# Four local edits in a one-core hybrid layer: the norm's weight row, the first gather, the last two experts

## The chip, the cores and the metric

The kernel runs on one core of a Trainium2 chip. The metric is the device time of one execution in microseconds. The kernel before has a median of 1229.29 us over 3 runs (1228.64 to 1230.97).

## The reference

One layer on 256 tokens of width 1024, all in fp32:

```python
h = rms_norm(x, mix_norm)
proj = h @ w_in                       # 1024 -> u | v | z | xBC | dt | gate_a | gate_b
y_a = sgu_branch(proj[u, v])          # chunk-causal gMLP
y_b = mamba2_branch(proj[z], proj[xBC], proj[dt], ...)
merged = sigmoid(gate_a) * (y_a @ w_branch_a) + sigmoid(gate_b) * (y_b @ w_branch_b)
x = x + merged @ w_out
x = x + moe_ffn(rms_norm(x, ffn_norm))    # top 4 of 32 experts, hidden 1024, clamped SwiGLU
x = x + sigmoid(rms_norm(x, ple_norm) @ w_ple_gate) * (p @ w_ple_proj)
return rms_norm(x, final_norm)
```

Each of the 32 experts has w1 (1024 x 2048) and w2 (1024 x 1024) in fp32, 12 MB together.

## The kernel before, in words

Tokens lie on partitions in two tiles (t = 0, 1) of 128. Five instruction streams are written out by hand and meet only in semaphores; the order in the source is the order on the engine. There is no scheduler.

**Head.** SP loads the norm's weight row (4 KB, one partition), the two tiles of x, and then the input projection's weights in halves of 1 MB. ScalarE (ACT) squares a tile with a running sum and takes the root (L1315, L1318). TensorE (PE) multiplies a row of ones with the weight row (L755), which puts the row on all partitions in two PSUM banks, between two stretches of matmuls whose result nobody reads (`keep_busy`, L747). VectorE (DVE) multiplies x by the inverse root and by those banks (L1642). PE transposes the result in four units ("xT", t, h) of four 128x128 blocks (L699). ACT copies each unit out as the high part `a_hi` (L1344), VectorE subtracts to get the low part `a_lo` (L1625). `a_hi` lies in the memory of `x`, so all of x must have been read before it is written. Each weight is split likewise: ACT rounds (L1307), GpSimd (POOL) subtracts (L669). The convolution's part of the projection ("xbc") then runs in groups of 8 matmuls per term: L777 (high x high), L787 (low activations), L782 (low weights). From there to the router, PE works through projections, branches and merge.

**Router and first gather.** VectorE turns the router's ranks into one-hot selections (`select`, L1937). PE gathers the up to 64 chosen rows per expert as a matmul of x with the selection (`gather`, L982, 8 k-tiles by 2 token tiles into bank YB), VectorE multiplies by the norm's weight (`take_gathered`, L1942), and expert 0 begins.

**Experts.** The weights come in 6 chunks of 2 MB per expert, (e, 0) to (e, 3) of w1 and (e, 4), (e, 5) of w2, into 9 slots. SP issues chunk g when chunk g-9 has been used (`chunk_used`). Chunks 0 to 5 are issued while the branches still run, 6 to 8 when the last part of the output projection is done (`wait_filled(sp, ("wo", 1, 1))`), chunk 9 when expert 0's first chunk has been used. Per expert PE does `units_of` (w1, L1032, bias L1038), the turn of the activation (L1061), the scatter of an earlier expert's output into four accumulators (L1002), the turn of its selection (L1009) and `rows_out` (w2, L1070) into bank YB, which ACT copies to memory (L1499, L1522).

**The last two experts** share an order of their own, `last_two`: chunks arrive as (30, 0 to 3), (31, 0 to 3), (30, 4), (30, 5), (31, 4), (31, 5). After that come the last scatter (L1167), the per-layer gate (L1280 and after) with weights that SP loads once (31, 4) has landed (L624), and the final norm.

## Time and profile before

| what | value |
|---|---|
| median of 3 runs | 1229.29 us |
| the profiled execution's own time | 1227.98 us |
| its span | 1226.2 us |
| TensorE busy | 1167.1 us (95%) |
| VectorE / ScalarE / GpSimd busy | 394.3 / 224.8 / 45.1 us |
| moved by DMA | 459.60 MB, 375 GB/s on average |
| chain that ended last | PE 68%, DMA 27%, VectorE 2%, ScalarE 2% |
| expert chunks, issue to landing | 36.0 us (median) |

The chain is followed back from the last instruction to what released it each time. A busy PE does not mean that PE sets the pace: where PE and DMA run side by side, the chain names DMA only in the stretches where PE waited for a landing. The span is 1.8 us shorter than the execution's own time, and that execution is 1.3 us below the median.

### The profile page before, as it was taken

The numbers are of one execution on the slowest core, as the hardware profiler recorded it, in microseconds if no ns is written. First come the engines' busy times: TensorE is split into PE (matmuls) and PEld (weight loads), VectorE is DVE, ScalarE is ACT, GpSimd is POOL, SyncE is SP. The second block draws the span as 40 slices with busy tenths as digits, with TensorE's granted clock in tenths as the row PEclk, the third lists the DMA queues.
The fourth block names the chain that finished last, engine by engine and source line by source line (L and its number), as shares of the span: only waits on it lengthen the run. The fifth ranks groups of instructions, "written<-read, shape, count | busy, mean of one in ns | idle before, by whom it ended". The sixth has DMA issues, their size and how long they took to land.

```text
span 1226.2 us, 14127 instructions
## 1 busy us (share of the span) xinstructions
PE 1167.1 (95%) x5773; PEld 586.7 (48%) x5773; DVE 394.3 (32%) x716; ACT 224.8 (18%) x338; POOL 45.1 (4%) x32
## 2 busy tenths in 40 slices
PE   9999999999999999999998989899999999999997
PEld 8988888874343443434332423233343333233336
DVE  2679954653221232122121212212222121212127
ACT  5766654350000000000000000000000000000017
POOL 6600000010000000000000000000000000000000
PEclk9999999999999999999999999999999999999999
DMA  8655478789999999999999999999999999999991
GB/s 271 203 172 206 137 275 334 266 304 403 430 427 427 429 428 428 429 428 428 429 428 429 430 429 428 429 426 428 427 427 428 428 428 428 429 428 427 428 391 46
DMA packets 62382, 459.60 MB, mean 375 GB/s; under 512 B 7385, under 2 KB 16993, under 8 KB 37506
## 3 DMA queue, kind: packets, MB, share of 16 engines
q1 hardware_dynamic: 62338, 458.95, 91.0%
q8 instruction: 35, 0.57, 0.2%
q14 instruction: 9, 0.07, 0.0%
HBM read 457.87 MB, written 1.06 MB: 374 GB/s over the span
## 4 chain that ended last, share of the span: by engine, by line
PE 68%; DMA 27%; DVE 2%; ACT 2%; issue 1%; ACTq 0%; SPq 0%; DVEq 0%
PE bank L1032 22%; DMA wring<-in_w_dram 15%; PE bank L1070 13%; DMA vz<-in_w_dram 12%; PE bank L712 5%; PE bank L714 5%; PE bank L713 5%; PE bank L993 4%; PE bank L1002 3%; PE bank L1038 2%; PE bank L777 1%; PE bank L782 1%; PE bank L787 1%; PE bank L699 1%; PE bank L1061 1%
## 5 line engine op out<-in xcount | busy, mean ns | idle before, releaser
L1032 PE MATMUL bank<-wring,hT 128*64 128x512 f32 x1360 | 310.4, 599 | 21.0 <-DMA wring<-in_w_dram 17.5
L1032 PEld LDWEIGHTS bank<-wring,hT 128*64 128x64 f32 x1360 | 94.1, 137 | 210.6 <-issue 171.9
L1985 DVE TENSOR_SCALAR xbcT<-bank 128x512 f32<-128x512 f32 x32 | 22.1, 692 | 526.4 <-PE bank L1038 526.4
L1070 PE MATMUL bank<-wring,xbcT 128*64 128x512 f32 x672 | 150.7, 595 | 7.3 <-DVE xbcT L2004 6.3
L1494 ACT ACTIVATE xbcT<-xbcT 128x512 f32<-128x512 f32 x32 | 20.2, 630 | 489.3 <-DVE xbcT L1985 489.3
L1070 PEld LDWEIGHTS bank<-wring,xbcT 128*64 128x64 f32 x672 | 46.5, 137 | 101.4 <-issue 91.7
L1632 DVE TENSOR_TENSOR blk_lo<-blk,blk_hi 128x2048 fp32r<-128x2048 f32 x32 | 73.0, 2287 | 39.5 <-ACT blk_hi L1309 39.5
L1032 PE MATMUL bank<-vz,hT 128*64 128x512 f32 x336 | 78.7, 599 | 7.1 <-DMA vz<-in_w_dram 7.1
L1499 ACT ACTIVATE xbcT<-bank 128x512 f32<-128x512 f32 x31 | 18.5, 597 | 352.5 <-PE bank L1070 352.5
L1032 PE MATMUL bank<-blk,hT 128*64 128x512 f32 x352 | 79.7, 594 | 3.2 <-DMA blk<-in_w_dram 3.2
L1070 PE MATMUL bank<-blk,xbcT 128*64 128x512 f32 x320 | 72.6, 595 | 3.1 <-DVE xbcT L2004 3.1
L712 PE MATMUL bank<-blk_hi,a_lo 128*128 128x512 f32 x192 | 75.5, 393 | 0.1
L714 PE MATMUL bank<-blk_lo,a_hi 128*128 128x512 f32 x192 | 74.8, 389 | 0.0
L713 PE MATMUL bank<-blk_hi,a_hi 128*128 128x512 f32 x192 | 74.7, 389 | 0.0
L1309 ACT ACTIVATE blk_hi<-blk 128x2048 fp32r<-128x2048 f32 x32 | 61.1, 1917 | 73.8 <-DMA blk<-in_w_in_dram 44.4
L1002 PE MATMUL bank<-xbcT 64*128 64x512 f32 x248 | 61.6, 615 | 0.7 <-ACT xbcT L1522 0.7
L2006 DVE COPY xbcT<-bank 128x256 f32<-128x256 f32 x32 | 13.4, 420 | 138.2 <-PE bank L1009 138.2
L1032 PEld LDWEIGHTS bank<-blk,hT 128*64 128x64 f32 x352 | 24.9, 137 | 54.3 <-issue 46.8
L1032 PEld LDWEIGHTS bank<-vz,hT 128*64 128x64 f32 x336 | 22.3, 136 | 51.2 <-issue 38.8
L993 PE MATMUL bank<-hT,ga 128*128 128x128 f32 x240 | 46.4, 275 | 0.0
L993 PE MATMUL bank<-xbcT,ga 128*128 128x128 f32 x240 | 46.3, 275 | 0.0
L1070 PEld LDWEIGHTS bank<-blk,xbcT 128*64 128x64 f32 x320 | 22.3, 137 | 48.4 <-issue 44.3
(300 smaller groups left out, 1215.2 us busy)
## 6 DMA issues: line engine op xcount, KB each, us to landing
wring<-in_w_dram SPq DMA_DIRECT2D x129, 2048.0 KB, 36.0
blk<-in_w_dram SPq DMA_DIRECT2D x42, 2048.0 KB, 35.5
vz<-in_w_dram SPq DMA_DIRECT2D x21, 2048.0 KB, 35.9
blk<-in_w_in_dram SPq DMA_DIRECT2D x28, 1024.0 KB, 5.2
blk<-in_w_branch_a_dram SPq DMA_DIRECT2D x4, 1024.0 KB, 5.5
blk<-in_w_branch_b_dram SPq DMA_DIRECT2D x4, 1024.0 KB, 8.1
blk<-in_w_out_dram SPq DMA_DIRECT2D x4, 1024.0 KB, 5.2
x<-in_x_dram SPq DMA_DIRECT2D x4, 512.0 KB, 5.3
```

Source lines behind the costliest of these rows:

```text
L712: mm(out, lhs[1], rhs[0], start=start, stop=False)
L713: mm(out, lhs[0], rhs[0], start=False, stop=False)
L714: return mm(out, lhs[0], rhs[1], start=False, stop=stop)
L993: last = mm(bank[:, k * P:(k + 1) * P], xp[:, t, (4 * h + k) * P:(4 * h + k + 1) * P], sel[t], start=(t == 0), stop=(t == TT - 1))
L1002: last = mm(ACC[t][dh][:, :], selgT[dh * SLOTS:(dh + 1) * SLOTS, t, :], y_sb[dh * SLOTS:(dh + 1) * SLOTS, :], start=False, stop=True, skip ...
L1032: last = mm(bank[dh * SLOTS:(dh + 1) * SLOTS, :], xgT[:, k, :], at(c)[:, kk * 2 * F + off + dh * W:kk * 2 * F + off + (dh + 1) * W], start ...
L1038: return mm(bank[:, :], esel[:, :], b1_pair[:, g * W:(g + 1) * W], start=False, stop=True, skip_group_check=True)
L1070: last = mm(YB[dh * SLOTS:(dh + 1) * SLOTS, :], units[:, kk * P + c * SLOTS:kk * P + (c + 1) * SLOTS], at(W1C + c)[:, kk * D + dh * W:kk * ...
L1309: fn(high(i), blk[:, i % NB, :], ACT.Copy).then_inc(blk_high, 1)
L1494: fn(sig_sb, g_sb, ACT.Sigmoid, scale=ALPHA).then_inc(msig_done, 1)
L1632: tt(blk_lo[:, i % NB, :], blk[:, i % NB, :], high(i).bitcast(FP32), ALU.subtract).then_inc(nat_low, 1)
L1985: ts(g_sb, GLU[:, :], LIMIT, None, ALU.min).then_inc(g_done, 1)
```

## The change

Four edits, with no change to what is computed:

1. The norm's weight row is loaded onto all 128 partitions by its DMA (512 KB written in place of 4 KB), between the two tiles of x. The two matmuls L755 go, and the two stretches of `keep_busy` become one of twelve matmuls. x goes into `ga` at first (`x_first`), so that `a_hi` can be written while the second tile is still being read; ACT and VectorE take up the transposed units one by one.
2. The router's gather is written in two halves of four k-tiles into two banks (YB, TB), and VectorE takes each half apart. It waits for the copy of the turned gates, which held TB.
3. Expert 30's `units_of` carries three quarters of expert 31's gather between its chunks; the last quarter follows it.
4. Expert 31's rows go into bank LIN, its first w2 chunk ahead of expert 30's scatter, and its last chunk is loaded in two DMAs.

```diff
-        mix_row = z[0:1, 0, :]
+        mix_gain = z[:, 0, :]
+        x_first = ga
...
-            load(mix_row, mix_norm, mix_loaded)
-            for t in range(TT):
-                load(x[:, t, :], x_in[0, t * P:(t + 1) * P, :], x_loaded[t])
+            for t in range(TT):
+                load(x_first[:, t, :], x_in[0, t * P:(t + 1) * P, :], x_loaded[t])
+                if t == 0:
+                    load(mix_gain, vec(mix_norm), mix_loaded)
...
+                elif g < NCH * E - 1:
+                    load(slots[g % NSLOT], chunk_src(*LAST_TWO[g - NCH * (E - 2)]), loaded[g % NSLOT])
                 else:
-                    load(slots[g % NSLOT], chunk_src(*LAST_TWO[g - NCH * (E - 2)]), loaded[g % NSLOT])
+                    for k in range(2):
+                        part = slice(k * RW2 // 2 * D, (k + 1) * RW2 // 2 * D)
+                        load(slots[g % NSLOT][:, part], chunk_src(E - 1, NCH - 1)[:, part], last_half[k])
...
-            keep_busy(idle_bank, 6, halves[:], halves[:])
+            keep_busy(idle_bank, 12, halves[:], halves[:])
             pe.wait_ge(consts, 2)
-            pe.wait_ge(mix_loaded, 16)
-            for h in range(HALVES):
-                last = mm(banks[(6 + h + BANK_SHIFT) % BANKS][:, :], ones[0:1, :], mix_row[:, h * W:(h + 1) * W], start=True, stop=True)
-            last.then_inc(gain_spread, 1)
-            keep_busy(idle_bank, 6, halves[:], halves[:])
...
+                    if first and RW1 * c == KT // 2:
+                        pe.wait_ge(xg_done, 1)
...
-            def rows_out(units, at, arrived, between=None):
+            def rows_out(units, at, arrived, between=None, to=YB, halved=False):
 
                 for c in range(W2C):
-                    arrived(W1C + c)
+                    if not (halved and c):
+                        arrived(W1C + c)
                     for kk in range(RW2):
+                        if halved and c and kk % 2 == 0:
+                            pe.wait_ge(last_half[kk // 2], 16)
...
-                units_of(first, *stream(first), 0)
-                gather(last_chosen)
+                def rows_between(c):
+
+                    gather(last_chosen if c == 0 else lambda: None, range(2 * c, 2 * c + 2))
+
+                units_of(first, *stream(first), 0, between=rows_between)
+                gather(lambda: None, range(6, KT))
...
-                pe.wait_ge(y_copied, first + 1)
-                scatter(lambda: None)
-                selected(GLU)
+                def first_scattered(c):
+
+                    pe.wait_ge(y_copied, first + 1)
+                    scatter(lambda: None)
+                    selected(GLU)
+
                 pe.wait_ge(actT_done, second + 1)
-                rows_out(actT_last, *stream(second))
+                rows_out(actT_last, *stream(second), between=first_scattered, to=LIN, halved=True)
...
+                pe.wait_ge(gateT_done, 1)
...
-            gather(first_ready)
+            first_ready()
+            for h, bank in enumerate((YB, TB)):
+                for k in range(4):
+                    for t in range(TT):
+                        last = mm(bank[:, k * SLOTS:(k + 1) * SLOTS], xp[:, t, (4 * h + k) * P:(4 * h + k + 1) * P],
+                                  sel[t][:, 0:SLOTS], start=(t == 0), stop=(t == TT - 1))
+                last.then_inc(first_rows if h == 0 else gathered, 1)
...
-            split(0, [0])
-            act.wait_ge(xn_done, 2 * TT)
-            high_parts("xT", a_hi)
+            for t in range(TT):
+                for h in range(2):
+                    if (t, h) == (1, 1):
+                        split(0, [0])
+                    name = ("xT", t, h)
+                    wait_filled(act, name)
+                    fn(a_hi[:, 4 * h:4 * h + 4, t * P:(t + 1) * P], seg4(bank_of(name)[:, :]), ACT.Copy).then_inc(act_high, 1)
...
-            take_y(E - 1)
+            act.wait_ge(chunk_used, NCH * E)
+            fn(y_sb, LIN[:, :], ACT.Copy).then_inc(y_copied, 1)
...
-            dve.wait_ge(gain_spread, 1)
-            for t in range(TT):
+            dve.wait_ge(mix_loaded, 16)
+            for t in range(TT):
+                if t:
+                    first_low(0)
                 dve.wait_ge(root_done, t + 1)
                 link(nc.vector.reciprocal(rstd[:, t:t + 1], rstd[:, t:t + 1]))
                 for h in range(HALVES):
                     cols = slice(h * W, (h + 1) * W)
-                    stt(v[:, t, cols], x[:, t, cols], rstd[:, t:t + 1], banks[(6 + h + BANK_SHIFT) % BANKS][:, :], ALU.mult,
+                    stt(v[:, t, cols], x_first[:, t, cols], rstd[:, t:t + 1], mix_gain[:, cols], ALU.mult,
                         ALU.mult).then_inc(xn_done, 1)
-            low_parts("xT", a_hi, a_lo, 0)
+            for n in range(1, 4):
+                first_low(n)
```

The first rows on ScalarE, before (`a_hi` is the high part of a transposed unit, `blk_hi1` that of a weight half):

```order
L1315 ACTIVATE u,ssq<-x 128x1024
L1318 ACTIVATE rstd<-ssq,eps 128x1
L1315 ACTIVATE u,ssq<-x 128x1024
L1318 ACTIVATE rstd<-ssq,eps 128x1
L1307 ACTIVATE blk_hi1<-blk 128x8x128
L1344 ACTIVATE a_hi<-bank6 128x4x128
L1344 ACTIVATE a_hi<-bank7 128x4x128
L1344 ACTIVATE a_hi<-bank0 128x4x128
L1344 ACTIVATE a_hi<-bank1 128x4x128
```

and now:

```order
L1339 ACTIVATE u,ssq<-ga 128x1024
L1342 ACTIVATE rstd<-ssq,eps 128x1
L1339 ACTIVATE u,ssq<-ga 128x1024
L1342 ACTIVATE rstd<-ssq,eps 128x1
L1377 ACTIVATE a_hi<-bank6 128x4x128
L1377 ACTIVATE a_hi<-bank7 128x4x128
L1377 ACTIVATE a_hi<-bank0 128x4x128
L1331 ACTIVATE blk_hi1<-blk 128x8x128
L1377 ACTIVATE a_hi<-bank1 128x4x128
```

The first weight half's rounding has moved from ahead of all four copies to a place ahead of the fourth.

PE from expert 30's second w2 chunk to the end of expert 31, before (bank6 is YB, banks 0 to 3 the accumulators):

```order
L1070 MATMUL bank6<-wring,xbcT 64x512 x8
L1002 MATMUL bank0<-xbcT 128x512
L1002 MATMUL bank1<-xbcT 128x512
L1002 MATMUL bank2<-xbcT 128x512
L1002 MATMUL bank3<-xbcT 128x512
L1009 MATMUL bank4<-ident,xbcT 128x128 x2
L1070 MATMUL bank6<-wring,hT 64x512 x16
```

and now (bank5 is LIN):

```order
L1080 MATMUL bank6<-wring,xbcT 64x512 x8
L1080 MATMUL bank5<-wring,hT 64x512 x8
L1004 MATMUL bank0<-xbcT 128x512
L1004 MATMUL bank1<-xbcT 128x512
L1004 MATMUL bank2<-xbcT 128x512
L1004 MATMUL bank3<-xbcT 128x512
L1011 MATMUL bank4<-ident,xbcT 128x128 x2
L1080 MATMUL bank5<-wring,hT 64x512 x8
```

The eight matmuls of chunk (31, 4) now stand ahead of expert 30's scatter; those of (31, 5) stay behind it.

## Rows read from the trace of the kernel before

**Rows 1.** The page, part 2: what the DMA engines moved, 40 slices.

```profile
GB/s 271 203 172 206 137 275 334 266 304 403 430 427 427 429 428 428 429 428 428 429 428 429 430 429 428 429 426 428 427 427 428 428 428 428 429 428 427 428 391 46
```

**Rows 2.** Chain that ended last, in order of time: start us, us, what.

```profile
1.38 2.93 PE bank L747 x12
4.31 3.71 PE bank L755 x4
8.02 2.86 PE bank L747 x12
10.88 2.57 PE bank L699 x12
13.47 1.19 ACT a_hi L1344 x2
14.71 1.22 PE bank L777 x8
...
17.85 0.96 PE bank L777 x8
...
1109.56 37.13 DMA vz<-in_w_dram
```

**Rows 3.** Timeline, first 30 us: start us, us, engine, line, operation [idle before <-releaser].

```profile
1.21 0.84 SPq L512 DMA_DIRECT2D x<-in_x_dram  x2
...
4.94 1.06 ACT L1315 ACTIVATE u<-x 128x1024 f32<-128x1024 f32 x1 [2.01 <-DMA x<-in_x_dram]
...
7.48 0.29 ACT L1318 ACTIVATE rstd<-ssq,eps 128x1 f32<-128x1 f32 x1
...
8.05 0.16 DVE L1639 RECIPROCAL rstd<-rstd 128x1 f32<-128x1 f32 x1 [5.16 <-PE bank L755]
8.25 1.41 DVE L1642 SCALAR_TENSOR_TENSOR vz<-x,rstd,bank 128x512 f32<-128x512 f32 x2
...
9.28 1.06 ACT L1307 ACTIVATE blk_hi<-blk 128x1024 fp32r<-128x1024 f32 x1 [1.50 <-DMA blk<-in_w_in_dram]
...
14.10 1.29 DVE L1625 TENSOR_TENSOR a_lo<-bank,a_hi 128x512 fp32r<-128x512 f32 x2 [0.16 <-ACT a_hi L1344]
...
15.68 16.59 POOL L669 TENSOR_TENSOR blk_lo<-blk,blk_hi 128x1024 fp32r<-128x1024 f32 x7 [2.91 <-ACT blk_hi L1307]
```

**Rows 4.** Line L699 (transposes): count, duration ns min/median/max, first and last start.

```profile
L699 PE MATMUL bank<-ident,vz x32: 270/273/421, 10.7 to 207.5; 128*128 128x128 f32 x32
```

**Rows 5.** Windows of 2 us; the last three numbers are clock, DMA share, GB/s.

```profile
282.00:284.00 2.00, 2.00 (x12) 0.81 (x10) 1.69 (x7) 0.00 (x0) 0.00 (x0) 1.00 1.07 360
284.00:286.00 2.00, 2.00 (x12) 0.86 (x10) 0.00 (x0) 0.00 (x0) 0.00 (x0) 1.00 0.69 254
```

**Rows 6.** Timeline of SP's queue, 195 to 345 us: issues of expert chunks.

```profile
267.69 22.11 SPq L548 DMA_DIRECT2D wring<-in_w_dram  x4
```

**Rows 7.** Chain that ended last, around expert 0's start.

```profile
274.30 3.79 PE bank L982 x32
278.09 0.83 issue
278.92 13.10 PE bank L1032 x60
```

**Rows 8.** Timeline, 255 to 300 us: VectorE's copy of the turned gates.

```profile
274.16 0.41 DVE L1954 COPY hT<-bank 32x256 f32<-32x256 f32 x1
```

**Rows 9.** Timeline of PE, 1130 to 1197 us.

```profile
1141.84 3.65 PE L1032 MATMUL bank<-wring,hT 128*64 128x512 f32 x16 [1.24 <-DMA wring<-in_w_dram]
...
1176.67 3.65 PE L1070 MATMUL bank<-wring,xbcT 128*64 128x512 f32 x16
1181.02 1.99 PE L1002 MATMUL bank<-xbcT 64*128 64x512 f32 x8 [0.70 <-ACT xbcT L1522]
...
1183.31 7.09 PE L1070 MATMUL bank<-wring,hT 128*64 128x512 f32 x32
```

**Rows 10.** Timeline of SP's queue, after 1000 us: the first gate weight loads.

```profile
1181.59 0.93 SPq L512 DMA_DIRECT2D vz<-in_w_ple_gate_dram  x2
```

More of the change, by code:

```diff
@@ L320, in build @@
         mix_loaded = sem("mix_loaded")
-        gain_spread = sem("gain_spread")
+        first_rows = sem("first_rows")
+        last_half = [sem(f"last_half{k}") for k in range(2)]
         ssm_loaded = sem("ssm_loaded")
@@ L1026, in units_of @@
                 xgT = xgT_of[0 if alone else 1 - side]
-                pe.wait_ge(xg_done, j + 1 + (not alone and side == 1))
+                if first:
+                    pe.wait_ge(first_rows, 2)
+                else:
+                    pe.wait_ge(xg_done, j + 1 + (not alone and side == 1))
                 def inner(c, kk, bank, off):
@@ L1062, in turned_units @@
                 last.then_inc(actT_filled, 1)
-            def rows_out(units, at, arrived, between=None):
+            def rows_out(units, at, arrived, between=None, to=YB, halved=False):
                 for c in range(W2C):
-                    arrived(W1C + c)
+                    if not (halved and c):
+                        arrived(W1C + c)
                     for kk in range(RW2):
+                        if halved and c and kk % 2 == 0:
+                            pe.wait_ge(last_half[kk // 2], 16)
                         for dh in range(2):
-                            last = mm(YB[dh * SLOTS:(dh + 1) * SLOTS, :], units[:, kk * P + c * SLOTS:kk * P + (c + 1) * SLOTS],
+                            last = mm(to[dh * SLOTS:(dh + 1) * SLOTS, :], units[:, kk * P + c * SLOTS:kk * P + (c + 1) * SLOTS],
                                       at(W1C + c)[:, kk * D + dh * W:kk * D + (dh + 1) * W],
@@ L1314, in _ @@
                 act.wait_ge(x_loaded[t], 16)
-                fn(u[:, t, :], x[:, t, :], ACT.Square, accum_out=ssq[:, t:t + 1]).then_inc(ssq_done, 1)
+                fn(u[:, t, :], x_first[:, t, :], ACT.Square, accum_out=ssq[:, t:t + 1]).then_inc(ssq_done, 1)
                 act.wait_ge(ssq_done, t + 1)
@@ L1635, in _, with first_low @@
             tt(dsel[:, :], ident[0:2 * HEADS, 0:HEADS], ident[0:2 * HEADS, HEADS:2 * HEADS], ALU.add).then_inc(small_set, 1)
-            dve.wait_ge(gain_spread, 1)
+            def first_low(n):
+                t, h = divmod(n, 2)
+                dve.wait_ge(act_high, n + 1)
+                cols = (slice(None), slice(4 * h, 4 * h + 4), slice(t * P, (t + 1) * P))
+                name = ("xT", t, h)
+                tt(a_lo[cols], seg4(bank_of(name)[:, :]), a_hi[cols].bitcast(FP32), ALU.subtract).then_inc(empty(name), 1)
+            dve.wait_ge(mix_loaded, 16)
             for t in range(TT):
+                if t:
+                    first_low(0)
                 dve.wait_ge(root_done, t + 1)
@@ L1958, in _ @@
                 cp(onehot[rows, 0:E], ident[rows, rows])
-            dve.wait_ge(gathered, 1)
-            take_gathered()
+            for h, (bank, done) in enumerate(((YB, first_rows), (TB, gathered))):
+                dve.wait_ge(done, 1)
+                tt(xgT_of[0][:, 4 * h:4 * h + 4, :], bank[:, 0:4 * SLOTS].rearrange("p (k s) -> p k s", k=4),
+                   fgain[:, 4 * h:4 * h + 4].unsqueeze(2).to_broadcast([P, 4, SLOTS]),
+                   ALU.mult).then_inc(xg_done if h else first_rows, 1)
             for t in range(TT):
```

## The prediction

> **What bounds the kernel now.** I read the page's DMA line first. The reader is to see that the expert stream runs flat from the eleventh slice to the last but one: 426 to 430 GB/s, slice after slice [rows 1]. A stretch that flat is DMA at its limit, although PE is busy 95% of the span. The chain that ended last agrees late in the stream: one step of it is 37.13 us of DMA that ends at 1146.69 [rows 2], the landing of chunk (30, 3). So three things can move the end: when the flat stretch begins, gaps in it, and what is left after its last chunks land. Edits 1 and 2 bear on the first two, edits 3 and 4 on the third.
>
> When does it begin? Chunks 6 to 8 are issued when the output projection is done (the row at 267.69 begins with chunk 8) [rows 6]. Up to there the chain is PE from 14.71 us on, group of matmuls behind group of matmuls [rows 2], so an earlier start of "xbc" moves the stream by as much. A gap stands right behind: in 282 to 286 us DMA moves 360 and then 254 GB/s [rows 5]. Against 428 that is 2 x 68/428 + 2 x 174/428 = 0.3 + 0.8 = 1.1 us lost. It is the wait for chunk 9, which goes out only when expert 0, begun at 278.92 [rows 7], has used its first chunk, 16 of 60 records in 13.10 us or 3.5 us later; chunks 6 to 8 have run out by then.
>
> **Edit 1, the head.** Before, the chain is keep-busy 2.93, the row's matmuls 3.71, keep-busy 2.86, twelve transposes 2.57, two high copies 1.19, then "xbc" at 14.71 [rows 2]. VectorE had waited 5.16 us for the row's matmuls [rows 3]. These go. What is late next?
> - Landings. x's first tile lands at 4.9 [rows 3]; issued one DMA sooner (0.84 for two, so 0.4 each) it lands at 4.5 to 4.9. The weight row now brings 512 KB; at about 420 GB/s that is 1.25 us, so it lands at 5.8 to 6.2 and the second tile at 7.1 to 7.5. No row shows this load in this place.
> - Square to root took (7.48 + 0.29 - 4.94)/2 = 1.4 us a tile [rows 3]. First root at 6.0 to 6.4, first norm (1.41 for two halves [rows 3]) done at 7.6 to 8.0; second root at 8.5 to 8.9.
> - ACT's first two high copies (0.6 each [rows 2]) end at 9.7 to 10.1. VectorE's first low part (1.29/2 = 0.65 [rows 3]) now stands ahead of the second tile's norm: low part to 9.8 to 10.2, reciprocal 0.2, first half of the norm 0.7: 10.7 to 11.1.
> - The third unit's four transposes at 2.57/12 = 0.21 us each take 0.85: 11.6 to 12.0. Its copy 0.6, then the rounding of the first weight half (1.06 [rows 3]) that now stands ahead of the fourth copy, then that copy 0.6: 13.9 to 14.3. The weight half itself lands 1 to 1.3 us later than at 9.28 [rows 3], by 10.6, and is not waited for.
>
> "xbc" would begin 0.4 to 0.8 us sooner. POOL gives part of it back: its first subtraction waits for that rounding, now done at 13.3 instead of 10.3, and one takes 16.59/7 = 2.37 us [rows 3], so the second low part is ready at 18.0. PE asks for it after four groups, 1.06 + 3 x 0.96 = 3.9 us [rows 2] from 13.9, at 17.8: 0.2 us. The small loads behind the weight row come about 1.3 us later too; ACT and POOL have room there, since PE wants the fifth weight half only at 14.7 + 4 x 5.8 = 38 us. Value 0.4 us gained. Bounds from the nearest rows: all 3.71 of the row's matmuls gained above; below, a loss, if PE's clock is lower where "xbc" begins (a rival).
>
> **Edit 2, the first gather.** It starts at 274.16 + 0.41 = 274.57 instead of 274.30 [rows 7, 8], since it now waits for the gates' copy: 0.3 lost. Its 32 records take 3.6 us as before, but the first half is through VectorE while the second runs, so the 0.83 us between last matmul and expert 0 goes [rows 7]. Expert 0 starts at about 278.2, 0.7 sooner, and chunk 9 is issued 0.7 sooner, inside the gap of 1.1. Value 0.7; bounds 0 (no gap of that cause) and 1.1 (the gap).
>
> **Edit 3.** PE stood 1.24 us idle before each of expert 30's later chunks [rows 9], and a quarter of the gather is about 0.9 us, so three quarters cost nothing there and 2.7 us leave the stretch behind them. But they are not collected: VectorE's chain to the activation stays, and whatever PE gains must wait for the next landings. PE takes up (30, 5) at 1176.67 [rows 9], and a chunk of 2.1 MB takes 4.9 us at 428 GB/s: six of those after 1146.69 is 1176.1, so it had hardly landed. (31, 4) landed just before 1181.59, where SP, which waits for it, issues the gate's loads [rows 10]. Value 0; bounds 0 and 0.7 (the other wait named below).
>
> **Edit 4.** Before, PE waited 0.70 us for the copy of expert 30's rows, began the scatter at 1181.02 and had no wait until the rows of 31 were done at 1190.4 [rows 9]: 9.4 us of work. After, the same work begins with (31, 4). PE is done with (30, 5) at 1180.3, must wait for the landing at about 1181.55, and then has 9.4 us ahead. The last chunk, 4.9 us behind, lands at 1186.4 and is asked for at 1187.2, so loading it in halves buys nothing. Against the stream this end is 0.5 us later. Bounds: 0.7 gained (the copy's wait gone, were (31, 4) there) and 0.6 lost.
>
> The reader who knows the page DMA: Bandwidth & Descriptors of the Trainium skill (section "Why a DMA increments its semaphore by 16 and not by 1") finds there that up to 16 engines finish a DMA independently and the wait is for all. By that rule the last engine counts, however much the others have moved, which speaks against edit 4; by a mean rate over all engines, seven steps of 4.9 after 1146.69, (31, 4) would be there at 1181.0 and the edit would cost nothing. SP's row, a real waiter on that chunk, decides for the first.
>
> **The sum.** -0.4 - 0.7 + 0 + 0.5 = -0.6 us against the profiled execution, 1227.98 (span 1226.2 and 1.8 around it), which gives 1227.4. That execution was 1.3 below the median 1229.29; on the median's scale I predict 1228.7.
>
> **Rivals.**
> - *The clock.* The transposes of the head took 421 ns, later ones 273 [rows 4], and 0.21 us apart against 0.11: PE's head ran on the lower of its two levels (1.2 and 2.4 GHz), though the granted clock reads 1.00, and it had risen by 14.71, after PE had been busy without a break since 1.38. After, PE stands idle about 2 us before the third unit and 2 before "xbc". If it is still at 1.2 GHz then, each group of 8 costs 0.96 more. Three groups: 1228.7 + 2.9 = 1231.6. From four on it is slower by more than the bound. For it: the gaps are new. Against: they are short and follow twelve matmuls on all rows; PE's 1.24 us gaps in the experts cost it no pace, 3.65 us for 16 records [rows 9]. TensorE: Matmul & The Clock Gate of the Trainium skill (Part 1, the HAM clock gate) says that the lower clock is the default and sustained activity releases it; by that rule the new order could also rise sooner.
> - *The clock, the other way.* It rises at the end of the unbroken keep-busy near 7.2 us. The third unit's transposes then take 0.44 instead of 0.85: 0.4 more, 1228.3.
> - *The tail is not held by (31, 4).* If PE finds it landed, the copy's 0.7 is gained where I charge 0.5: 1227.5. For it: PE was busy then, so none of its rows shows the landing. Against: SP's issue.
> - *The stream does not start sooner.* The gap is the queue's own and the head's gain is eaten by later loads: only the 0.5 stays, 1229.8.
>
> **How the numbers follow.** My forecast 0.44, clock low 0.10, clock early 0.22, tail free 0.12, stream fixed 0.12. The range for 8 in 10 covers all but the low clock's far end and adds the spread of a median of this kernel: 1226.9 to 1231.0. I take 0.2%, 2.5 us, as what can be told from no change. None of the faster cases reaches it alone; two together, with the head's upper bound, might: 0.07. The low clock does from four groups on, and unforeseen waits might: 0.09. Within: 0.84.
>
> **What would show it.** Right: "xbc" begins at 13.8 to 14.3 with the next groups at 0.96; expert 0 starts 0.7 sooner counted from the last output projection; the gap near 284 is about 0.4; PE idles about 1.2 us ahead of (31, 4) and the last rows end 9.4 us after its landing. Wrong: groups of 1.9 us at the start of "xbc"; a weight row that lands after 7 us; the chain passing from SP's queue to something else in the experts; (31, 4) used without a wait.

## The result: slower by 2.9 us

| kernel | median | runs | ratio, 95% interval |
|---|---|---|---|
| before | 1228.71 us | 12 | 1 |
| after | 1231.61 us | 12 | 1.0018 [1.0010, 1.0026] |
| after, timed a second time | 1231.42 us | 12 | 1.0026 [1.0013, 1.0038] |

The forecast was 1228.7, range 1226.9 to 1231.0: the time lies outside, on the side of the rival with the low clock (1231.6). The two medians are 2.9 us apart; the ratios, which pair runs of the same rounds, make it 2.2 us [1.2, 3.2] and 3.2 us [1.6, 4.7]. With twelve runs the kernel before has a median 0.6 below the 1229.29 of three runs on whose scale the forecast was put; on the new scale the forecast would be 1228.1. The profiled execution of after took 1231.88 us, its span is 1230.1, so it is 3.9 us longer than that of before.

The DMA line of the page of after is as flat as before from the eleventh slice on [rows 1]: the stream runs at the same rate, only later.

```profile
GB/s 281 207 169 209 137 250 357 245 303 406 428 429 427 427 428 427 430 427 428 429 429 428 428 429 428 428 427 428 426 429 427 427 427 429 428 426 428 427 377 37
```

**The head.** The timeline of PE in the kernel after, first 20 us (start us, us, engine, line, operation, [idle before <-what ended it]):

```profile
1.37 4.51 PE L754 MATMUL bank<-halves 128*128 128x128 f32 x24 [1.37 <-DVE halves L1643]
7.59 1.23 PE L706 MATMUL bank<-ident,vz 128*128 128x128 f32 x8 [1.71 <-DVE vz L1680]
11.45 1.94 PE L706 MATMUL bank<-ident,vz 128*128 128x128 f32 x8 [2.63 <-DVE vz L1680]
14.66 2.07 PE L779 MATMUL bank<-a_hi,blk_hi 128*128 128x256 f32 x8 [1.27 <-ACT a_hi L1377]
16.53 1.91 PE L789 MATMUL bank<-a_lo,blk_hi 128*128 128x256 f32 x8
18.24 1.16 PE L784 MATMUL bank<-a_hi,blk_lo 128*128 128x256 f32 x8
```

The same view of the kernel before, its first and its fourth group of "xbc":

```profile
14.71 1.22 PE L777 MATMUL bank<-a_hi,blk_hi 128*128 128x256 f32 x8 [0.69 <-ACT a_hi L1344]
...
17.69 1.12 PE L777 MATMUL bank<-a_hi,blk_hi 128*128 128x256 f32 x8
```

The chain of after has the fourth group as

```profile
19.40 0.96 PE bank L779 x8
```

and windows of 1 us of after (the last three numbers are granted clock, DMA share, GB/s):

```profile
11.00:12.00 1.00, 0.55 (x3) 0.56 (x4) 1.00 (x3) 0.00 (x0) 0.00 (x0) 0.76 1.10 347
12.00:13.00 1.00, 1.00 (x7) 0.99 (x5) 0.66 (x2) 0.43 (x1) 0.00 (x0) 0.50 1.12 343
...
18.00:19.00 1.00, 1.00 (x10) 1.00 (x8) 0.00 (x0) 1.00 (x2) 1.00 (x2) 0.83 1.10 342
```

The reader is to see four things. The 24 records of the products that nobody reads take 4.51 us where 24 at the old pace would be 5.86 [twice 2.93, rows 2]: the clock rises from 1.2 to 2.4 GHz inside them. Then PE idles 1.71 us, 2.63 us and 1.27 us, with 1.23 and 1.94 us of transposes between. Between 11 and 12 us the granted clock falls (0.76 over that window), and from 12 to 18 us it reads 0.50, the lower level. So "xbc" begins at 14.66, no later than before (14.71), but its first three groups take 2.07, 1.91 and 1.16 us, where in the same view of before they take 1.22, 1.12 and 1.12. A row of the timeline ends after the next has begun; in the chain of waits, where nothing is counted twice, a group at full pace is 0.96. There the fourth group begins at 19.40 instead of 17.85 [rows 2]: 1.55 us.

**Up to the stream.** PE then waits once more where before it did not, for the low part of "v"'s first weight half; and SP issues chunk 6 at 269.15. Timelines of PE and SP, kernel after:

```profile
65.24 0.47 PE L719 MATMUL bank<-blk_hi,a_lo 128*128 128x512 f32 x1 [0.68 <-DVE blk_lo L1661]
```

```profile
269.15 0.35 SPq L551 DMA_DIRECT2D wring<-in_w_dram  x1
```

Before, chunk 6 went out at 266.83: the stream's first chunks go out 2.32 us later, 1.55 + 0.68 + 0.09.

**The router.** Chain of waits of after, around expert 0's start, and PE's timeline there:

```profile
276.58 0.40 issue
276.98 3.75 PE bank L1206 x32
280.74 2.29 PE bank L1037 x9
```

```profile
280.67 10.52 PE L1037 MATMUL bank<-wring,hT 128*64 128x512 f32 x48
```

The 0.83 ahead of expert 0 is gone and 0.40 stands ahead of the gather [rows 7]. By the timeline expert 0 starts at 280.67 (the chain puts it 0.07 later), 1.75 later than at 278.92, so 0.57 of the 2.32 came back, where the forecast had 0.7.

**The tail.** Timelines of PE and of SP's queue at experts 30 and 31, kernel after:

```profile
1157.76 0.63 PE L1068 MATMUL bank<-ident,xbcT 128*128 128x128 f32 x4 [1.83 <-DVE xbcT L2034]
1158.31 3.68 PE L1004 MATMUL bank<-xbcT 64*128 64x512 f32 x8
...
1162.30 3.65 PE L1037 MATMUL bank<-wring,hT 128*64 128x512 f32 x16
...
1184.84 3.60 PE L1080 MATMUL bank<-wring,hT 128*64 128x512 f32 x16
1188.38 1.99 PE L1004 MATMUL bank<-xbcT 64*128 64x512 f32 x8
...
1195.02 1.99 PE L1184 MATMUL bank<-xbcT 64*128 64x512 f32 x8 [0.70 <-ACT xbcT L1552]
```

```profile
1184.62 0.93 SPq L514 DMA_DIRECT2D vz<-in_w_ple_gate_dram  x2
```

Expert 30's scatter takes 3.68 us instead of 1.99; (31, 4) is taken up at 1184.84 without a wait; SP, who waits for the same chunk, issues the gate's loads 3.03 later than at 1181.59 [rows 10]; and the last scatter begins 10.40 us behind SP's issue, before 1191.09 - 1181.59 = 9.50. The sum: 2.32 (up to the stream) - 0.57 (router) + 1.28 (the stream, from expert 0 to (31, 4)) + 0.90 (tail) = 3.93 us, the difference of the last scatters.

### The profile page after: what moved, and what is told of

It reads as the page before. It is cut to its first block, busy times and chain, and to the rows that moved or that the text cites. A ratio compares the mean times of both kernels' runs of the same rounds, so it can differ in the third digit from the quotient of the medians.

```text
span 1230.1 us, 14122 instructions
## 1 busy us (share of the span) xinstructions
PE 1164.9 (95%) x5769; PEld 585.4 (48%) x5769; DVE 394.2 (32%) x717; ACT 224.5 (18%) x338; POOL 45.1 (4%) x32
## 3 DMA queue, kind: packets, MB, share of 16 engines
HBM read 458.39 MB, written 1.06 MB: 373 GB/s over the span
## 4 chain that ended last, share of the span: by engine, by line
PE 65%; DMA 28%; DVE 4%; ACT 2%; issue 1%; SPq 0%; ACTq 0%; DVEq 0%
PE bank L1037 21%; DMA wring<-in_w_dram 15%; PE bank L1080 13%; DMA vz<-in_w_dram 12%; PE bank L719 5%; PE bank L721 5%; PE bank L720 5%; PE bank L995 4%; PE bank L1004 2%; PE bank L1043 2%; PE bank L779 1%; PE bank L789 1%; PE bank L1068 1%; PE bank L784 1%; PE bank L706 1%
## 5 line engine op out<-in xcount | busy, mean ns | idle before, releaser
L1080 PEld LDWEIGHTS bank<-blk,xbcT 128*64 128x64 f32 x320 | 22.3, 137 | 48.4 <-issue 44.3
```

The costliest lines, as they stand in the source:

```text
L1080: last = mm(to[dh * SLOTS:(dh + 1) * SLOTS, :], units[:, kk * P + c * SLOTS:kk * P + (c + 1) * SLOTS], at(W1C + c)[:, kk * D + dh * W:kk * ...
```

## The experiments

Fifteen runs besides before and after, two of them of these same kernels again. Chunk 6, expert 0 and the last scatter are starts in us in each one's own trace; "(31, 4)" is SP's issue of the gate's loads, which waits for that chunk.

| kernel | ratio [95%] | first "xbc" group | chunk 6 | expert 0 | (31, 4) | last scatter |
|---|---|---|---|---|---|---|
| before | 1 | 14.71 | 266.83 | 278.92 | 1181.59 | 1191.09 |
| before again | 0.9999 [0.9989, 1.0008] | 12.46 | 265.09 | 277.18 | 1179.84 | 1189.89 |
| only edit 1 | 1.0033 [1.0021, 1.0045] | 14.30 | 268.65 | 280.73 | 1184.48 | 1194.53 |
| only edit 2 | 0.9986 [0.9977, 0.9995] | 14.95 | 267.40 | 278.93 | 1181.97 | 1192.02 |
| only edit 3 | 1.0007 [0.9997, 1.0017] | 14.06 | 266.26 | 278.35 | 1182.36 | 1193.06 |
| only edit 4 | 1.0010 [1.0001, 1.0018] | 12.41 | 265.05 | 277.13 | 1179.35 | 1189.64 |
| edits 2, 3, 4 | 0.9996 [0.9987, 1.0005] | 14.19 | 266.48 | 278.00 | 1180.58 | 1190.87 |
| after | 1.0018 [1.0010, 1.0026] | 14.66 | 269.15 | 280.67 | 1184.62 | 1195.02 |
| after again | 1.0026 [1.0013, 1.0038] | 14.60 | 268.68 | 280.21 | 1184.24 | 1194.59 |
| after, head filled | 1.0010 [1.0001, 1.0019] | 14.34 | 268.76 | 280.29 | 1182.64 | 1192.98 |
| after, tail filled | 1.0015 [1.0006, 1.0025] | 14.70 | 269.16 | 280.68 | 1183.31 | 1193.60 |
| edit 1, head filled | 1.0011 [1.0002, 1.0020] | 14.15 | 268.37 | 280.46 | 1183.35 | 1193.39 |
| before + 512 KB | 1.0007 [0.9998, 1.0016] | 14.37 | 268.67 | 280.75 | 1183.87 | 1193.91 |
| edit 1, small load | 1.0022 [1.0013, 1.0031] | 13.64 | 267.79 | 279.88 | 1185.15 | 1195.23 |
| same, head filled | 1.0013 [1.0004, 1.0022] | 13.79 | 268.03 | 280.11 | 1183.61 | 1193.69 |
| row late | 0.9998 [0.9987, 1.0009] | 13.10 | 265.50 | 277.59 | 1179.70 | 1189.74 |
| row late + edit 2 | 0.9995 [0.9986, 1.0004] | 13.50 | 266.07 | 277.60 | 1180.36 | 1190.40 |

### One edit at a time

The kernel before with edit 1 alone:

```diff
+                    load(mix_gain, vec(mix_norm), mix_loaded)
...
-            keep_busy(idle_bank, 6, halves[:], halves[:])
+            keep_busy(idle_bank, 12, halves[:], halves[:])
...
-            act.wait_ge(xn_done, 2 * TT)
-            high_parts("xT", a_hi)
```

> The kernel before with edit 1 alone (weight row spread by its load, head reordered). Theory A (clock): PE idles between 5.9 and 11.4 us, the granted clock falls to half and stays there over the first groups of "xbc", which then take about 1.9 us each; that costs 1.5 us, and weight halves that land later cost about 0.7 more at "v". Chunk 6 is issued 2.0 to 2.5 us later than before and the program ends 1.8 to 2.8 us later. Rival B (my forecast): "xbc" begins 0.4 sooner, end 0.4 sooner. Rival C (clock without lasting cost): the 1.5 us are absorbed by a wait for weights further on, end within 0.5 of before.

Measured: 1.0033, which is 4.0 us [2.6, 5.5]: the whole loss and more. Theory A's place is there (groups of 2.08 and 1.91 us from 14.30 on, windows at clock 0.50), chunk 6 goes out 1.82 later than in the trace of before, and my forecast's 0.4 sooner is refuted.

Its complement, after with edit 1 undone (the weight row by PE's products with ones, the old order of VectorE and ACT):

```diff
-            keep_busy(idle_bank, 12, halves[:], halves[:])
+            keep_busy(idle_bank, 6, halves[:], halves[:])
...
+            last.then_inc(gain_spread, 1)
+            keep_busy(idle_bank, 6, halves[:], halves[:])
```

> The kernel after without edit 1: edits 2, 3 and 4 stay. If edit 1 is the whole loss (theory A), the stream starts about 0.5 us sooner than before (edit 2) and the end is -0.6 to +0.3 us from before. If the tail edits cost about 0.9 us by themselves (theory T: the scatter of expert 30 runs at half clock and nothing hides it), the end is +0.4 us or later. The scatter of expert 30 should take 3.7 us instead of 2.0 in both, since the wait ahead of it is there in both.

Measured: 0.9996, so without edit 1 the change costs nothing. Of the scatter I was wrong: here it took 1.99 us behind the same idle 1.83. And PE waits for (31, 4), as forecast. Timeline of PE, edits 2, 3 and 4:

```profile
1153.66 0.63 PE L1072 MATMUL bank<-ident,xbcT 128*128 128x128 f32 x4 [1.83 <-DVE xbcT L2024]
1154.21 1.99 PE L1008 MATMUL bank<-xbcT 64*128 64x512 f32 x8
...
1180.65 3.65 PE L1084 MATMUL bank<-wring,hT 128*64 128x512 f32 x16 [1.33 <-DMA wring<-in_w_dram]
```

Edit 2 alone:

```diff
-            gather(first_ready)
+            first_ready()
+            for h, bank in enumerate((YB, TB)):
...
+                last.then_inc(first_rows if h == 0 else gathered, 1)
```

> The kernel before with edit 2 alone (router's gather in halves). Forecast and theory: expert 0 starts 0.5 to 0.7 us sooner counted from the issue of chunk 6, chunk 9 goes out sooner by as much, the DMA gap near 284 us shrinks and everything up to the tail is 0.5 us sooner; end -0.7 to -0.3. Rival: the gap is the queue's own; the stream's later chunks arrive as before, end 0.

Measured: 0.9986, 1.7 us [0.6, 2.8] faster, the only edit that gained. Its trace has expert 0 at 11.53 us behind chunk 6; over all kernels it is 11.52 to 11.53 with edit 2 and 12.08 to 12.09 without: 0.56 gained every time, the rest of the 1.7 is not in its trace (whose execution took 1228.88, 1.1 above the kernel's median).

Edit 3 alone:

```diff
-                units_of(first, *stream(first), 0)
-                gather(last_chosen)
+                units_of(first, *stream(first), 0, between=rows_between)
+                gather(lambda: None, range(6, KT))
```

> The kernel before with edit 3 alone (the gather of expert 31's rows in four parts between expert 30's chunks). Theory T: PE idles about 1.8 us after the last quarter, the granted clock falls and the scatter takes 3.7 us instead of 2.0; expert 31 starts about 1 us sooner than before instead of 2.7; the end is within 0.4 us of before, because PE must wait for chunk landings anyway. Rival: no fall of the clock when DMA's waits lie elsewhere, scatter 2.0, expert 31 starts 2.5 to 2.9 sooner, end again the same. Slower by more than 0.8 us would say that landings do not hold PE in the tail at all.

Measured: 1.0007, no difference that can be told. Timeline of PE and a window, only edit 3:

```profile
1155.09 0.66 PE L1061 MATMUL bank<-ident,xbcT 128*128 128x128 f32 x4 [1.83 <-DVE xbcT L1996]
1155.68 3.60 PE L1002 MATMUL bank<-xbcT 64*128 64x512 f32 x8
...
1159.58 1.94 PE L1032 MATMUL bank<-wring,hT 128*64 128x512 f32 x8
```

```profile
279.00:280.00 1.00, 1.00 (x4) 0.27 (x2) 0.89 (x3) 0.00 (x0) 0.00 (x0) 0.50 1.03 442
```

Counted from the second bias product of expert 30 (1151.92 here, 1150.91 before), expert 31 starts 7.66 us later against 6.67 before: the scatter takes 3.60. (I had expected it about 1 us sooner; it is 1 us later.) In the trace of edits 2, 3 and 4, where the clock held, it is 6.01 (from 1150.49), and the half clock is the difference of 1.6: edit 3 is worth 0.66 us of PE's time, not the 2.7 of three quarters of the gather, since VectorE's chain leaves 1.83 of them idle. This trace has a surprise elsewhere: the clock is at 0.50 where expert 0 starts, a stretch that edit 3 doesn't touch. SP's chunk 9 goes out at 283.69, 17.43 us behind chunk 6, where in before it is 15.77 (282.60): 1.66 us of the stream that are not the edit's.

Edit 4 alone:

```diff
-                rows_out(actT_last, *stream(second))
+                rows_out(actT_last, *stream(second), between=first_scattered, to=LIN, halved=True)
```

> The kernel before with edit 4 alone (scatter of expert 30 behind chunk (31, 4), expert 31's rows in LIN, last chunk in halves). My forecast: PE waits at about 1180.3 until (31, 4) lands at 1181.5, and the end is 0.5 us later than before. Rival: the chunk is there, the 0.7 us wait for ACT's copy goes, end 0.7 us sooner. Both lie inside 0.1%, so the trace decides: an idle stretch of PE ahead of the first product with (31, 4) and whether the last rows end 9.4 us behind it.

Measured: 1.0010, 1.2 us [0.1, 2.2] slower. Timeline of PE and SP's queue, only edit 4:

```profile
1145.07 2.79 PE L1037 MATMUL bank<-vz,hT 128*64 128x512 f32 x12 [1.25 <-DMA vz<-in_w_dram]
...
1179.42 3.65 PE L1078 MATMUL bank<-wring,hT 128*64 128x512 f32 x16 [0.81 <-DMA wring<-in_w_dram]
1183.00 1.99 PE L1007 MATMUL bank<-xbcT 64*128 64x512 f32 x8
...
1189.64 1.99 PE L1178 MATMUL bank<-xbcT 64*128 64x512 f32 x8 [0.70 <-ACT xbcT L1535]
```

```profile
1179.35 0.93 SPq L513 DMA_DIRECT2D vz<-in_w_ple_gate_dram  x2
```

PE waits 0.81 for the landing in place of 0.70 for ACT's copy, and the last scatter begins 10.29 behind it. In the kernels with the old order it is 9.50 once (before), 10.70 once (only edit 3) and 10.04 to 10.08 in all nine others. In those nine SP issues within 0.03 of the start of the scatter. That looks like one releasing the other, but both stand at a fixed distance from an earlier landing, that of (30, 3), for which PE waits in all these traces (the first row above; at 1147.69 in only edit 2, at 1146.74 in before). In ten of the eleven traces in which PE waits there, SP issues 34.25 to 34.29 us behind PE's start on (30, 3); this one, in which PE itself waits for (31, 4), has 34.28. Seven steps of 4.9 us, the forecast's time of a chunk, are 34.3. So SP's issue marks the landing. Only in before it is 34.85, 0.57 later. Counted from the same start, the last scatter begins at 44.57 us here and at 44.31 to 44.35 in the others, before among them: edit 4 costs 0.24 us by the traces (forecast: 0.5). Against an execution with the late landing, like the one from which I took it, it would by an estimate have cost 0.8 (10.29 against 9.50). The interval of the ratio holds both.

### Is it the clock or the bytes?

Edit 1 does two things: it leaves PE idle in the head and it puts 512 KB in front of the weights. After, with products that nobody reads put into the waits:

```diff
-            keep_busy(idle_bank, 12, halves[:], halves[:])
+            keep_busy(idle_bank, 19, halves[:], halves[:])
...
+                    if (t, h) == (1, 0):
+                        keep_busy(idle_bank, 11, halves[:], halves[:])
                     pe.wait_ge(xn_done, 2 * t + h + 1)
...
+            keep_busy(idle_bank, 5, halves[:], halves[:])
             pe.wait_ge(act_high, 4)
```

> The kernel after with products that nobody reads put into PE's waits of the head (7 more in the first run of them, 11 ahead of the second tile's transposes, 5 ahead of "xbc"). Theory A (clock): the granted clock stays at 1.00 through 11 to 19 us, the first groups of "xbc" take 0.96 us, and the end is 1.3 to 2.0 us sooner than the kernel after (229.9 to 230.4 over 1000). Rival C: the later weight landings hold PE anyway, and less than 0.5 us comes back.

The same filling with edit 1 alone:

> The kernel before with edit 1 alone and products that nobody reads in PE's waits of the head (7, 11 and 5 more). Edit 1 alone gave 1.0033. Theory A (clock): its 1.5 us of groups at half clock go, ratio 1.0018 to 1.0024, granted clock 1.00 from 11 to 19 us. Rival C (late weights): nothing comes back, ratio 1.003.

Measured: 1.0010 against 1.0018 for after, and 1.0011 against 1.0033 for edit 1 alone: 1.0 and 2.7 us come back. For after the two intervals overlap, for edit 1 alone they don't. In both traces the clock is 1.00 throughout and the first groups take 1.21 and 1.12 us in the timeline, as before. Timelines of PE and ACT, after with the head filled:

```profile
14.34 1.21 PE L782 MATMUL bank<-a_hi,blk_hi 128*128 128x256 f32 x8 [0.34 <-ACT a_hi L1380]
15.39 1.12 PE L792 MATMUL bank<-a_lo,blk_hi 128*128 128x256 f32 x8
```

```profile
119.16 0.47 PE L719 MATMUL bank<-blk_hi,a_lo 128*128 128x512 f32 x1 [1.29 <-ACT u L1418]
```

```profile
116.18 1.91 ACT L1336 ACTIVATE blk_hi<-blk 128x2048 fp32r<-128x2048 f32 x1 [7.18 <-DMA blk<-in_w_in_dram]
```

The seventeen traces agree on what the low clock costs. From the first group of "xbc" to the first matmul of "v" it is 48.4 to 48.9 us in the eight with the old order and no extra load, 50.2 to 50.7 in the six with edit 1 or an extra load and nothing filled, and 49.0 to 49.1 in the three with a filled head.

But PE's row at 119.16 shows what neither theory had: a new wait of 1.29 us behind two copies of ACT (L1418) that stand behind its rounding of a weight half. It is there in all three kernels with a filled head (1.29, 1.28, 1.15) and in no other. ACT's row shows why the rounding is late: it waited 7.18 us for the half's landing. That landing came 8.8 to 9.0 us behind SP's issue in these three, 7.3 to 7.7 in the fourteen others. Why it took longer isn't settled. So chunk 6 of the two kernels above is only 0.4 and 0.3 us sooner than that of after and of edit 1 alone, although "xbc" runs at full pace, and the 1.0 and 2.7 us of the ratios are more than their traces show up to there.

One number of every execution, not only of the profiled one, bears on the cause: the granted clock as a mean over the whole span. Its median is 0.997 in before again and 0.996 with edits 2, 3, 4, but 0.991 in after, both times (0.988 to 0.995 over 24 executions; the trace read above has 0.994, less of the lower level than most), and 0.994 with edit 1 alone; with the head filled it is 0.996 and 0.997 again (0.995 to 0.998 over 22). So edit 1 lowers the clock and the filling gives it back over the executions as a whole, and not only in the profiled ones.

The other way round, the kernel before with the bytes alone:

```diff
                 load(x[:, t, :], x_in[0, t * P:(t + 1) * P, :], x_loaded[t])
+                if t == 0:
+                    load(z[:, 1, :], vec(mix_norm), small_loaded)
...
-            act.wait_ge(small_loaded, 16 * 7)
+            act.wait_ge(small_loaded, 16 * 8)
```

> The kernel before with one more load of 512 KB (the weight row spread over the partitions) behind x's first tile; nobody uses it. It leaves PE's order alone and delays everything behind it in SP's queue. Theory L (late landings cost 0.7 us of the loss): x's second tile, the weight halves and the small loads land about 1.2 us later, PE waits for "v" or later weights, chunk 6 is issued 0.5 to 1.2 us later. Rival (landings have room): the second tile's norm is 0.5 to 1 later at most and the end within 0.3 of before.

Measured: 1.0007, and chunk 6 goes out at 268.67. At first sight theory L. The timeline of PE and two windows say otherwise:

```profile
10.82 1.75 PE L701 MATMUL bank<-ident,vz 128*128 128x128 f32 x8 [1.56 <-DVE vz L1644]
14.37 2.07 PE L779 MATMUL bank<-a_hi,blk_hi 128*128 128x256 f32 x8 [1.80 <-ACT a_hi L1346]
16.25 1.91 PE L789 MATMUL bank<-a_lo,blk_hi 128*128 128x256 f32 x8
17.95 1.30 PE L784 MATMUL bank<-a_hi,blk_lo 128*128 128x256 f32 x8
```

```profile
12.00:13.00 1.00, 0.57 (x3) 0.17 (x1) 0.11 (x1) 1.00 (x3) 0.54 (x1) 0.50 1.09 344
17.00:18.00 1.00, 1.00 (x7) 1.00 (x7) 0.00 (x0) 0.72 (x2) 1.00 (x2) 0.50 1.10 348
```

The later second tile leaves PE idle 1.56 and 1.80 us, the clock falls, and the first three groups take 2.07, 1.91 and 1.30. By the chain the fourth begins 4.88 us behind the first, before 3.14 [rows 2]: 1.74 us. From the first group to chunk 6 it is 254.30 us here and 252.12 before, 2.18 more, so the clock is 1.74 of it and 0.44 I can't place. So in this execution the bytes acted through the clock: they made PE wait, and the clock fell.

Two things keep that from being edit 1's loss. The clock of this head had risen early (the row's matmuls took 2.20 us), and in the two traces of the old head that rose early "xbc" begins at 12.4 and 12.5 (below): against those the bytes also moved the start by 1.9 us. And the trace isn't the rule: its mean granted clock is 0.993, while seven of the eleven executions have 0.996 or 0.997, as before has. The median is 0.9 us [-0.2, 2.0] above before, where edit 1 alone costs 4.0 [2.6, 5.5].

Edit 1 with a load of 128 KB (32 partitions; the other 96 hold ones, the norm's weight is left out there):

```diff
-                    load(mix_gain, vec(mix_norm), mix_loaded)
+                    load(mix_gain[0:32, :], mix_norm.rearrange("a n -> (a n)").partition_broadcast(32), mix_loaded)
...
+                nc.vector.memset(mix_gain[32 * q:32 * q + 32, :], 1.0).then_inc(gain_spread, 1)
```

> Edit 1 alone, but the weight row is loaded to 32 partitions (128 KB instead of 512) and the other 96 hold ones, so the norm's weight is left out there. Theory B (bytes): x's second tile lands 0.9 us sooner, the head is sooner by as much, weights land sooner, and most of the loss goes: ratio 1.000 to 1.0015. Theory O (order and clock): PE still idles ahead of "xbc", the clock falls, groups of 1.9 us stay, ratio 1.0025 to 1.0035.

> The same with the products that nobody reads in PE's waits. Both theories expect a held clock. Theory B: the wait of 1.3 us at 119 us goes with the bytes, ratio 0.9985 to 1.0003. Theory O: it stays, ratio 1.0005 to 1.0015.

Measured: 1.0022 and 1.0013. With 384 KB fewer, "xbc" begins at 13.64 instead of 14.30, the clock is still at 0.50 there (groups of 2.08 and 1.76), and the ratio stays above 1.001. In this trace expert 0 too starts at the lower level: 0.50 from 280 to 282 us, and chunk 9 goes out 17.41 us behind chunk 6. The second keeps its wait of 1.15 at 118.41. Neither bears out theory B; 1.0022 also lies below theory O's 1.0025, though its interval reaches over it. Three quarters of the bytes gone return at most a third of the loss, with intervals that overlap (1.0013 to 1.0031 and 1.0021 to 1.0045).

### Two throws of the same programs

> The kernel after, unchanged. If its loss in the head is what its first trace shows, the granted clock is half at the start of "xbc" again, chunk 6 is issued at 268.5 to 269.5, and the ratio is 1.0018 within 0.1%. If the first trace was one throw of several, "xbc" starts at full clock this time.

Measured: 1.0026. "xbc" begins at 14.60 with groups of 2.08 and 1.74, the clock reads 0.50 in the windows read from 9 to 17 us, chunk 6 goes out at 268.68, and the scatter takes 3.67. The head's loss is no single throw.

> The kernel before, unchanged: what two samples of one program differ by, and one more trace of its head. Theory V (the clock's rise varies): in some executions of the old head the clock rises inside the row's products near 5 us and "xbc" begins at about 12.4 (the trace of edit 4 alone), in others at 10 us or later and "xbc" begins at 14.1 to 14.9 (four other traces); this trace shows one of the two, the times spread over 1226 to 1231, the ratio is 1.000 within 0.1%. Rival: the head always takes the same time, the 12.4 was a reading of another program, and this trace shows 14.7.

Measured: 0.9999, and a head of its own. Timeline of PE, the kernel before a second time:

```profile
4.24 2.25 PE L755 MATMUL bank<-vz,ones 1*128 1x512 f32 x4
6.42 1.60 PE L747 MATMUL bank<-halves 128*128 128x128 f32 x12
...
12.46 1.21 PE L777 MATMUL bank<-a_hi,blk_hi 128*128 128x256 f32 x8 [2.04 <-ACT a_hi L1344]
```

The row's four matmuls take 2.25 and the second run of products 1.60, where the chain of the first trace has 3.71 and 2.86 [rows 2]: the clock rose near 5 us, and "xbc" begins at 12.46, 2.25 sooner than in the trace on which I had built. The old head rises early in two of six traces (12.41, 12.46) and late in four (14.06 to 14.95); all are executions of identical instructions up to there. The mean issue of chunk 6 over these six is 266.19, over the four with edit 1's whole load and no fillers in the head 268.91: edit 1 costs 2.7 us by the traces, more than the 2.32 against one of them. The row at 12.46 shows one thing more: PE had waited 2.04 us, longer than two of after's three waits, and the group still took 1.21; the granted clock reads 1.00 throughout. One wait of that length, alone, didn't lower the clock.

Can the clock of the old head be made to rise early always?

```diff
-            keep_busy(idle_bank, 6, halves[:], halves[:])
+            keep_busy(idle_bank, 10, halves[:], halves[:])
...
-            keep_busy(idle_bank, 6, halves[:], halves[:])
+            keep_busy(idle_bank, 3, halves[:], halves[:])
```

> The kernel before with its head's products that nobody reads moved ahead of the weight row's: 10 and 3 instead of 6 and 6. Theory V: the products with one row of the array don't raise the clock reliably, ten on all rows do; the clock is up at 5 to 6 us in every execution, "xbc" begins at 12.5 to 13.3, and the median falls by 0.5 to 1.5 us. Rival: when the clock rises does not depend on which products run, and the head varies as before, ratio 1.000.

> The same head together with edit 2, the one edit that was faster by itself (0.9986). If both gains stand and add: 1226 to 1227 us, ratio 0.997 to 0.9985. If the head gives nothing: 0.9986 again.

Measured: 0.9998 and 0.9995, no difference. "xbc" begins at 13.10 and 13.50, but the clock rose early and fell again in both. Timeline of PE and a window, row late:

```profile
8.83 3.53 PE L699 MATMUL bank<-ident,vz 128*128 128x128 f32 x16 [0.17 <-DVE vz L1642]
```

```profile
10.00:11.00 1.00, 1.00 (x7) 0.90 (x6) 0.95 (x2) 0.48 (x2) 0.46 (x1) 0.50 1.09 348
```

Up to this row's end PE had waited nowhere longer than 0.2 us since 1.37, and yet the clock fell between 9 and 10 us. So a long wait isn't the only thing behind which it falls; what lowered it here isn't shown. The median of the second doesn't repeat edit 2's 0.9986 either; the two intervals overlap.

### The tail's scatter

```diff
                 pe.wait_ge(selT_done, first)
+                keep_busy(TB, 8, halves[:], halves[:])
                 turned_units(first)
```

> The kernel after with eight products that nobody reads put into the wait between the last quarter of the gather and expert 30's transposes. Theory T (clock): the granted clock stays up, the scatter of expert 30 takes 2.0 instead of 3.7 us and expert 31 starts 1.7 us sooner; since the landing of (31, 4) then holds PE, the end is 0 to 0.5 us sooner than the kernel after. Rival: the scatter still takes 3.7 us, because it is slowed by something else (the copies of ACT or VectorE), and nothing changes.

Measured: 1.0015, after 1.0018. Timeline of PE, after with the tail filled:

```profile
1154.42 2.00 PE L754 MATMUL bank<-halves 128*128 128x128 f32 x16
...
1156.94 1.99 PE L1004 MATMUL bank<-xbcT 64*128 64x512 f32 x8
...
1183.38 3.65 PE L1080 MATMUL bank<-wring,hT 128*64 128x512 f32 x16 [1.35 <-DMA wring<-in_w_dram]
```

Theory T holds: no idle, scatter 1.99. But what it saves turns into 1.35 us of waiting for (31, 4). In after the slow scatter made PE late enough to find the chunk landed, 0.22 behind SP's issue. The last scatter begins 10.40 behind that issue in after and 10.29 here, so the low clock in the tail costs 0.1 us and not 1.7.

## Why the prediction was wrong

- **"'xbc' would begin 0.4 to 0.8 us sooner"; value 0.4 gained.** This step failed. The start was close (14.66; the two low copies and the rounding stand in the order forecast), its pace was not. The rival "The clock" priced it rightly (three groups, 1231.6) and got 0.10, though its size was too large: it had 2.9 us for them. What the runs showed in place of the 0.4 gained is a loss: "xbc" starts at the lower level, and by the chain its first three groups take 1.55 us more than before in the trace of after, 1.43 to 2.35 in the other traces with edit 1 and no filled head, and less than 0.1 when the waits are filled. The argument that I had put against it, "they are short and follow twelve matmuls on all rows; PE's 1.24 us gaps in the experts cost it no pace", compared gaps and not what lies between them: in the experts 3.65 us of work stand between gaps of 1.24, in the head 1.23 us between 1.71 and 2.63. That this is the difference is my reading; it fits the one wait of 2.04 us behind an early rise, which cost under 0.2 us of pace, and doesn't cover the fall in row late. The Trainium skill, TensorE: Matmul & The Clock Gate (Part 1, the HAM clock gate), has the lower clock as the default that sustained activity lifts; by that rule an early rise promises nothing for later, and the trace agrees: up inside 1.37 to 5.88, down again at 11.
- **A small term beside it.** The 0.2 that POOL was to take back rests on a first group of 1.06, which is its distance from start to start in the timeline (14.71 to 15.77); the row cited has 1.22 [rows 2], and with it nothing is left of the 0.2.
- **The landings.** "The weight row lands at 5.8 to 6.2, the second tile at 7.1 to 7.5": VectorE took the row up at 6.50 and ACT the second tile at 7.85, 0.3 late each, by which PE's second idle was longer than the "about 2 us" of the rival. "The small loads come about 1.3 us later; ACT and POOL have room": nothing here showed a wait for them, but "v" waited 0.68 for a low part in after and 0.43 in after again, 0.35 with edit 1 alone; the old head has 0.17 to 0.41 in four of its six traces and none in two, so it belongs to no edit for certain.
- **The trace was one throw.** The sum was made against an execution whose clock rose late. That cost the forecast another 0.4 (2.7 against 2.3, by means of six and four traces) and hid that an early rise, on which I had set 0.22 as a gain of the change, was there before it in a third of the traces.
- **Edit 2, 0.7.** Right in mechanism, 0.56 in size. The second half's pass through VectorE costs nothing: expert 0 follows the gather without a gap (280.67). I had put the gather's 32 records at 3.6 us where the row has 3.79 [rows 7]; 274.57 + 3.79 = 278.36 is 0.56 sooner.
- **Edit 3, 0.** Right for the time. Unforeseen: the 1.83 us of idle of PE behind the last quarter, in which the clock can fall (in four of the five traces with edit 3 and no filler there: 3.60, 3.68, 3.67, 3.44; 1.99 in the fifth). The landing of (31, 4) hides nearly all of it.
- **Edit 4, 0.5 lost.** Right in sign, 0.24 in size. I had let SP's row decide against the mean rate, by which (31, 4) would be there at 1181.0; that row was the odd one, and the other ten traces bear out the mean rate (34.3 us behind (30, 3)). Yet the edit isn't free, as I had it by that rate. The wait is there whenever PE is on time (0.81, 1.33, 1.35). In after it wasn't, because the head and the scatter had made PE late: "(31, 4) used without a wait" was my sign for the rival "tail free", and it came true for a reason that has nothing to do with it.
- **Open.** 1.3 us of after's 3.93 arise between expert 0 and (31, 4) at an unchanged rate. That stretch takes 902.1 to 904.0 us in sixteen of the seventeen traces and 905.3 in the other (edit 1 with the small load). Part of the spread has a place: only edit 3 (904.0) and edit 1 with the small load have the clock at 0.50 where expert 0 starts, and chunk 9 goes out 1.65 us later behind chunk 6 in both than in the others without edit 2. The rest has none: kernels that are alike there differ by 1.3 (903.95 in after, 902.63 with its tail filled). I take it for the spread of the stream; no run shows its cause.

The only version whose interval lies wholly below 1 is the one with edit 2 alone, 0.9986 [0.9977, 0.9995]; with a changed head beside it, it was 0.9995 [0.9986, 1.0004], so the gain is small and was measured once.

## What to carry to other kernels

A wait that disappears from one engine's queue may have been the work that kept PE's clock up: price each new idle stretch of PE together with how little work stands between it and the next, and price the groups behind it at the lower level, not only at their own. One long wait alone didn't lower it here, and in one head it fell without any, so take it as a risk to be priced and not as a rule. Before a trace becomes the base of a sum of tenths, look at whether its clock rose where it usually does; two traces of one program can differ by more than the change. And filling the waits can bring the pace back without being the cure: by the traces, most of what it gave back here went into a later wait.

## Of the hardware

- The granted clock reads 1.00 in the first microseconds although the products there run at half pace (12 in 2.93 us, later 1.60); it reads 0.50 only once it has been up and fallen. The durations tell the level, not that column.
- The clock at one place varies between executions of the same instructions: at the head (rise near 5 us or at 10 and later), where expert 0 starts (0.50 in two of seventeen traces, within 278 to 282 us), and in expert 30's scatter. Runs of the kernel before lie between 1225.89 and 1231.66; the head's 2.3 us and the 1.65 where expert 0 starts are a part of that that the traces show.
- 384 KB more in front of it moved ACT's start on the second tile from 6.61 to 7.82, 1.21 us (edit 1 with the small load against edit 1).
